# Two feed-forward stages with seven-product pairs: eight plain pairs in the first, six in the second, and another order at entry and exit

## The reference

```python
def swiglu(x, w_gate, w_up, w_down):
    return (jax.nn.silu(x @ w_gate) * (x @ w_up)) @ w_down

h = h + 0.5 * swiglu(rms_norm(h, ffn1_norm[i]), ffn1_w_gate[i], ffn1_w_up[i], ffn1_w_down[i])
# attention and retention mixer
h = h + 0.5 * swiglu(rms_norm(h, ffn2_norm[i]), ffn2_w_gate[i], ffn2_w_up[i], ffn2_w_down[i])
```

## Time and profile before

| | us |
|---|---|
| median of three runs | 1853.77 |
| the three runs | 1857.15, 1853.77, 1852.72 |
| the profiled execution | 1852.79 |
| its span | 1851.0 |

### The profile page before, as it was taken

The page is one execution under the profiler, slowest core; times in us unless marked ns, Lnnn a source line. Parts: engine busy times, 40 slices in busy tenths (PEclk is TensorE's granted clock), DMA queues, the critical chain, the costliest instruction groups (busy, mean ns, idle before and its releaser), DMA issues.

```text
span 1851.0 us, 26244 instructions
## 1 busy us (share of the span) xinstructions
PE 1815.0 (98%) x9768; PEld 1535.0 (83%) x9768; DVE 1020.3 (55%) x1619; ACT 772.6 (42%) x1226; POOL 902.6 (49%) x678
## 2 busy tenths in 40 slices
PE   9899999999999999999899999999999999999998
PEld 8699988887888667888799988888877888888887
DVE  7977776225776654245876652257655375555312
ACT  6455553232332562234455542246344444444221
POOL 5444455486766524455434454353433454444542
PEclk9999999999999999999999999999999999999999
DMA  5233333253322312322233333242212222323331
GB/s 175 80 103 103 103 111 101 68 144 113 92 80 86 103 46 80 103 92 91 79 93 114 103 103 96 79 126 80 90 59 75 90 98 92 100 92 98 94 97 51
DMA packets 55195, 175.20 MB, mean 95 GB/s; under 512 B 6400, under 2 KB 10752, under 8 KB 55088
## 3 DMA queue, kind: packets, MB, share of 16 engines
q1 hardware_dynamic: 54848, 173.37, 29.9%
q10 hardware_dynamic: 240, 0.36, 0.1%
HBM read 166.63 MB, written 2.10 MB: 91 GB/s over the span
## 4 chain that ended last, share of the span: by engine, by line
PE 90%; DVE 6%; ACT 3%; issue 1%; POOL 0%; DVEq 0%; ACTq 0%; POOLq 0%
PE acc L2033 20%; PE acc L2035 20%; PE acc L2034 20%; PE acc L2233 6%; PE acc L2234 5%; PE acc L2238 5%; PE acc L2138 1%; PE acc L2140 1%; PE acc L2139 1%; DVE comb L1375 1%; DVE aux L1386 1%; DVE comb_raw L1358 1%; PE aux L2414 1%; ACT comb_raw L870 1%; PE acc L2564 1%
## 5 line engine op out<-in xcount | busy, mean ns | idle before, releaser
L710 POOL TENSOR_TENSOR w_lo<-w_raw,w_hi 128x512 fp32r<-128x512 f32 x498 | 671.5, 1372 | 698.8 <-ACT w_hi L817 698.7
L817 ACT ACTIVATE w_hi<-w_raw 128x1024 fp32r<-128x1024 f32 (+2 forms) x249 | 254.4, 1028 | 465.1 <-PE acc L2035 397.2
L2033 PE MATMUL acc<-u_hi,w_lo 128*128 128x512 f32 x1032 | 411.6, 399 | 0.3 <-DVE gcum L1907 0.2
L2035 PE MATMUL acc<-u_hi,w_hi 128*128 128x512 f32 x1032 | 402.1, 390 | 0.0
L2034 PE MATMUL acc<-u_lo,w_hi 128*128 128x512 f32 x1032 | 401.9, 389 | 0.0
L2233 PE MATMUL acc<-comb,w_hi 128*128 128x256 f32 x896 | 228.3, 286 | 20.0 <-ACT tmp L893 11.0
L730 POOL TENSOR_TENSOR w_lo<-w_raw,w_hi 128x512 fp32r<-128x512 f32 x96 | 133.8, 1394 | 212.3 <-ACT w_hi L883 212.3
L2033 PEld LDWEIGHTS acc<-u_hi,w_lo 128*128 128x128 f32 x1032 | 193.7, 188 | 49.6 <-issue 9.1
L2034 PEld LDWEIGHTS acc<-u_lo,w_hi 128*128 128x128 f32 x1032 | 193.8, 188 | 41.3 <-issue 2.6
L2035 PEld LDWEIGHTS acc<-u_hi,w_hi 128*128 128x128 f32 x1032 | 193.7, 188 | 41.1
L2234 PE MATMUL acc<-comb,w_hi 128*128 128x256 f32 x896 | 227.2, 285 | 0.0
(11 more groups left out here) (382 smaller groups left out, 3219.2 us busy)
## 6 DMA issues: line engine op xcount, KB each, us to landing
w_raw<-in_w_up SPq DMA_DIRECT2D x132, 512.0 KB, 3.6
w_raw<-in_w_mix SPq DMA_DIRECT2D x67, 512.0 KB, 3.6
w_raw<-in_w_down SPq DMA_DIRECT2D x48, 512.0 KB, 3.5
w_raw<-in_w_gla SPq DMA_DIRECT2D x30, 512.0 KB, 3.6
w_raw<-in_w_down SPq DMA_DIRECT2D x24, 384.0 KB, 3.1
w_raw<-in_w_ple SPq DMA_DIRECT2D x10, 512.0 KB, 3.8
tmp<-tmp SPq DMA_DIRECT2D x36, 64.0 KB, 2.0
h<-in_xT SPq DMA_DIRECT2D x8, 256.0 KB, 6.2
```

The source lines that it names most:

```text
L710: ins = pool.tensor_tensor(w_lo[:, slot, part], w_raw[:, slot, part], w_hi[:, slot, part].bitcast(F32), ALU.subtract)
L817: act.activation(w_hi[:, slot, 0:width], w_raw[:, slot, 0:width], ACT.Copy).then_inc(hi_ready, 1)
L2033: pe.matmul(o, w_lo[:, slot, columns], x_hi, start=first, stop=False)
L2035: return pe.matmul(o, w_hi[:, slot, columns], x_hi, start=False, stop=last)
```

## The change

`PLAIN` becomes `(8, 6)`, one number for each stage, `EARLY` becomes 8: in FFN1 the pairs 6 and 7 are plain, in FFN2 their products go to `hid_raw` as before but are split in periods 18 and 19 (`p - LAZY`) into places of their own. 14 late blocks are left in both, and the low ones lie in another order, so that the first four wait for product s1 and the next two for s3. The last plain pair's multiplication and its two parts move from ahead of the first period into it. At the exit `right_up` comes after two late blocks.

```diff
-PLAIN = 6
-EARLY = PLAIN
+PLAIN = (8, 6)
+EARLY = 8
...
-            return late_hi[:, k - EARLY, :], late_lo[:, (k - EARLY - 4) % LATE, :]
+            i = k - EARLY
+            return late_hi[:, i, :], late_lo[:, i + 2 if i < 4 else i - 4 if i < 6 else i, :]
...
+        LAZY = KF - EARLY - 2
...
@@ ACT, ffn_up
-                    hidden_hi(p, up_t[:, p % 2, :])
+                    if p < PLAIN[f] - 1:
+                        hidden_hi(p, up_t[:, p % 2, :])
...
+                    if p == PLAIN[f]:
+                        hidden_hi(p - 1, up_t[:, (p - 1) % 2, :])
+                    if PLAIN[f] <= p - LAZY < EARLY:
+                        late_hidden(p - LAZY)
                     left_gate(p)
...
-                split_comb("g1")
-                split_comb("s1")
-                split_slabs(n0 + 11)
-                split_comb("s2")
-                split_comb("s3")
-                plain_gate(3)
-                split_slabs(n0 + 12)
+                if f == 0:
+                    split_slabs(n0 + 11)
+                    plain_gate(3)
+                    split_slabs(n0 + 12)
+                    split_comb("g1")
+                    split_comb("s1")
+                    split_slabs(n0 + 13)
+                    plain_gate(4)
+                    split_slabs(n0 + 14)
+                    split_comb("s2")
+                    split_comb("s3")
+                    split_slabs(n0 + 15)
+                    plain_gate(5)
+                    split_slabs(n0 + 16)
+                else:
...
@@ DVE, ffn_up
-                def plain_pair(p):
+                def plain_evict(p):
...
+                def plain_pair(p):
+                    plain_evict(p)
                     plain_product(p)
+                    hidden_lo(p, up_t[:, p % 2, :])
...
                 def period(p):
...
+                    else:
+                        plain_product(p - 1)
                     if more:
                         sum_low(p + 1, "s2")
+                    if p == PLAIN[f]:
+                        hidden_lo(p - 1, up_t[:, (p - 1) % 2, :])
+                    if PLAIN[f] <= p - LAZY < EARLY:
+                        hidden_lo(p - LAZY, hid_raw[:, p - LAZY - PLAIN[f], :])
                     left_gate(p)
...
-                    if EARLY + 4 <= k < EARLY + 8:
-                        dve.wait_ge(q_done, q_count(f, KF - 1, "s1"))
-                    elif k >= EARLY + 8:
-                        dve.wait_ge(tile_done, t0 + 2 * (KF - 1) + (1 if k < EARLY + 12 else 2))
-                    hidden_lo(k, hid_raw[:, k - EARLY, :])
+                    if k < EARLY + 6:
+                        dve.wait_ge(q_done, q_count(f, KF - 1, "s1" if k < EARLY + 4 else "s3"))
+                    else:
+                        dve.wait_ge(tile_done, t0 + 2 * (KF - 1) + (1 if k < EARLY + 10 else 2))
+                    hidden_lo(k, hid_raw[:, k - PLAIN[f], :])
...
-                for of in ("g2", "s4", "u2"):
-                    split_comb(of)
-                plain_pair(5)
-                for p in range(PLAIN, KF):
+                split_comb("g2")
+                plain_evict(PLAIN[f] - 1)
+                split_comb("s4")
+                split_comb("u2")
+                for p in range(PLAIN[f], KF):
                     period(p)
-                for k in range(EARLY, EARLY + 6):
-                    late_hidden(k)
+                late_hidden(EARLY)
+                late_hidden(EARLY + 1)
                 right_up(KF - 1)
-                for k in range(EARLY + 6, EARLY + 12):
+                for k in range(EARLY + 2, EARLY + 8):
                     late_hidden(k)
                 left_up(KF - 1)
                 product(KF - 1)
-                for k in range(EARLY + 12, KF):
+                for k in range(EARLY + 8, KF):
                     late_hidden(k)
```

More of the change, by code:

```diff
@@ L531, in pair_no @@
         def pair_no(f, p):
-            return f * PAIRS + p - PLAIN
+            return sum(KF - PLAIN[e] for e in range(f)) + p - PLAIN[f]
         def q_count(f, p, of):
@@ L622, in _ @@
             sp.wait_ge(lo_ready, RING)
-            for n in range(RING, 2 * PLAIN):
+            for n in range(RING, 2 * PLAIN[0]):
                 load(n, A["w_up1"][n])
@@ L663, in _ @@
                     sp.dma_start(dec[:, :], A["decay"][step[1] + 1]).then_inc(dec_loaded, 16)
-            for n in range(2 * PLAIN):
+            for n in range(2 * PLAIN[1]):
                 load(plan.first["up2"][0] + n, A["w_up2"][n])
@@ L734, in lo_pairs @@
                 n0 = plan.first[name][0]
-                for p in range(PLAIN, KF):
+                for p in range(PLAIN[f], KF):
                     pool.wait_ge(half_hi, pair_no(f, p) + 1)
                     lo_unit(name, p, "g1").then_inc(half_lo, 1)
-                    if p > PLAIN:
+                    if p > PLAIN[f]:
                         pool.wait_ge(hi_ready, n0 + 2 * p)
@@ L905, in late_hidden @@
                 def late_hidden(k):
[L906 to L907 removed]
+                    if k >= EARLY:
+                        act.wait_ge(q_done, q_count(f, KF - 1, ("g1", "s2", "g2", "s3")[(k - EARLY) // 4]))
+                    hidden_hi(k, hid_raw[:, k - PLAIN[f], :])
                 def period(p):
                     more = p + 1 < KF
[L912 removed]
+                    if p > PLAIN[f]:
                         copy_part(p - 1, 3)
@@ L955, in ffn_up @@
                 split_slabs(n0 + 10)
-                split_comb("g1")
-                split_comb("s1")
-                split_slabs(n0 + 11)
-                split_comb("s2")
-                split_comb("s3")
-                plain_gate(3)
-                split_slabs(n0 + 12)
+                if f == 0:
[13 more added lines that the diff above has]
+                else:
+                    split_comb("g1")
+                    split_comb("s1")
+                    split_slabs(n0 + 11)
+                    split_comb("s2")
+                    split_comb("s3")
+                    plain_gate(3)
+                    split_slabs(n0 + 12)
                 for of in ("g2", "s4", "u2"):
                     split_comb(of)
-                unit_hi(PLAIN, "g1", half_hi)
-                unit_hi(PLAIN, "s2", sum_hi)
-                plain_gate(4)
-                unit_hi(PLAIN, "g2", hi_ready)
-                unit_hi(PLAIN, "s3", sum_hi)
-                for p in range(PLAIN, KF):
+                unit_hi(PLAIN[f], "g1", half_hi)
+                unit_hi(PLAIN[f], "s2", sum_hi)
+                plain_gate(PLAIN[f] - 2)
+                unit_hi(PLAIN[f], "g2", hi_ready)
+                unit_hi(PLAIN[f], "s3", sum_hi)
+                for p in range(PLAIN[f], KF):
                     period(p)
@@ L980, in ffn_up @@
                 split_slabs(d0 + 3)
-                for k in range(EARLY + 12, KF - 1):
-                    late_hidden(k)
+                late_hidden(KF - 2)
                 split_slabs(d0 + 4)
@@ L1457, in ffn_up @@
                     plain_product(0)
+                    hidden_lo(0, up_t[:, 0, :])
                 else:
@@ L1463, in ffn_up @@
                 combine()
[L1464 to L1478 removed]
+                if f == 0:
+                    plain_pair(3)
+                    split_comb("g1")
+                    split_comb("s1")
+                    plain_pair(4)
+                    split_comb("s2")
+                    split_comb("s3")
+                    plain_pair(5)
+                else:
+                    split_comb("g1")
+                    plain_pair(3)
+                    split_comb("s1")
+                sums_loaded(PLAIN[f])
+                for of in ("s3", "s1", "s2", "s4"):
+                    add(PLAIN[f], of)
+                if f == 1:
+                    split_comb("s2")
+                    split_comb("s3")
+                plain_pair(PLAIN[f] - 2)
+                sum_low(PLAIN[f], "s2")
+                sum_low(PLAIN[f], "s3")
+                split_comb("g2")
+                plain_evict(PLAIN[f] - 1)
+                split_comb("s4")
+                split_comb("u2")
+                for p in range(PLAIN[f], KF):
                     period(p)
[L1480 to L1481 removed]
+                late_hidden(EARLY)
+                late_hidden(EARLY + 1)
                 right_up(KF - 1)
[L1483 removed]
+                for k in range(EARLY + 2, EARLY + 8):
                     late_hidden(k)
@@ L2200, in ffn_up @@
                     f = k // 2
-                    for j in range(RING, 2 * PLAIN):
+                    for j in range(RING, 2 * PLAIN[f]):
                         fm_tile(t0 + j, [(n0 + j, b) for b in range(KD)], u_hi, u_lo)
@@ L2270, in up_end @@
                     multiply(p, "u2", "c", False).then_inc(tile_done, 1)
-                for p in range(PLAIN, KF - 1):
+                for p in range(PLAIN[f], KF - 1):
                     bank_a(p)
-                    if p > PLAIN:
+                    if p > PLAIN[f]:
                         gate_end(p - 1)
```

53 lines of the change are left out of this document (18 added, 35 removed).

## The result

| | before | after |
|---|---|---|
| median, us | 1853.77 | 1843.93 |
| lowest to highest of five runs | 1852.72 to 1857.15 | 1842.93 to 1844.93 |
| profiled execution | 1852.79 | 1844.09 |
| its span | 1851.0 | 1842.3 |

The ratio is 0.9945, with a 95% interval of 0.993 to 0.9959. The kernel became 9.8 us faster by the medians and 8.7 by the profiled executions; 13.8 were forecast. 1843.93 lies inside the range, 3.9 us above the predicted time.

The account below looks back on a forecast made before the run. PE, busy 98% of the span, was taken as the bound. FFN1 6.3, FFN2 3.3 and exits 6.8 make 16.4 us, less one clock fall of 2.6: 13.8 gained, 1840.0 us predicted, range 1835.5 to 1846.0.

Parts of the forecast that it names:

- the case with the greatest chance: At the two FFN entries, one fall of the clock costing 2.6 us, wait before s4 3.3: 1840.0 us, chance 0.42.
- the three signs of being wrong: s4's wait at the entries 4 us or more, the down projection waits, or FFN1's plain tiles show gaps.
- What bounds the kernel: PE is busy 98% of the span; only its work and the gaps in it move the end.
- The exits: Up-bank read moved ahead of late blocks at both FFN exits: 3.4 us gained twice, 6.8.
- DVE stands waiting in FFN1: At FFN1's entry two more plain pairs leave DVE 15 us against 7 us of delay, so it waits for the last tile.
- The wait before s4 ... becomes 3.3.: PE's wait for ACT's third copy at each entry falls from 4.34 to 3.3 us; bounds 2.5 and 4.3.
- The clock: At each entry an even chance of a fall to the low level, 2.6 us for each fall; one fall counted.
- the rival that both fall: Rival: the clock falls at both FFN entries, 1842.6 us; chance 0.20.
- the entries' chain isn't shortened: Rival: at both entries the hidden block eats the 2.25 us, s4's wait stays 4.34; 1844.0 us, chance 0.06.
- POOL's pressure should be over by then: 14 late blocks at the exits and into the down projection: priced at nothing, upper bound 1.7 us twice.
- where DVE and ACT wait for PE anyway: nothing: Splitting blocks 6 and 7 in FFN2's periods 18 and 19 costs nothing.
- The sum: FFN1 6.3, FFN2 3.3, exits 6.8, together 16.4 us, less one clock fall of 2.6: 13.8 us gained.

Follow-up runs that it names:

- the fastest version: Changed kernel with the hidden block's parts a period later, splits of s4 and u2 out of the way, FFN2's down slab split held: 1830.67 us.
- the repeat: The changed kernel itself run once more, nothing changed, for its time and the clock at both entries: 1843.8 us.

## Why the prediction was right, and by how much not

The gain was forecast, and the time lies in the range. But the case with the greatest chance (one fall of the clock, a wait of 3.3) did not come, and two of the three signs of being wrong did: s4's wait is 4.02, and the down projection waits. FFN1's plain tiles show no gap.

- *What bounds the kernel: right.* What was gained and lost are gaps of PE and its clock, to within 0.2 us of the 8.7; PE's own work grew by the 1.6 us worked out. That eight plain pairs pay more than this was right too, here by 4.2 us and in the fastest version by 5.6.
- *The exits: right, by 0.3 us.* 6.5 measured for 6.8. Undoing them costs 7.7, because those waits can bring the low clock as well, which the prediction's rows did not show.
- *DVE stands waiting in FFN1: right.* 4.75 us of idle time before its last plain tile.
- *What failed: "The wait before s4 ... becomes 3.3."* It was 4.02 and 4.03. The mis-sized term is the hidden block ahead of the left gate: 1.2 us forecast (ACT 0.55, DVE 0.6), 1.7 measured by taking it away. Of these DVE waited 0.34 for ACT's high part, and its own instruction took 1.34, since POOL's subtraction of g2 had begun 0.47 us earlier; with ACT's order turned round it took 0.68. The trace of before has such an instruction at 0.69 (913.98), where POOL was still for almost all of it, and it has POOL's subtraction just where the block was to go, behind DVE's low part of s2 at 920.83:

```profile
921.39 1.26 POOL L730 TENSOR_TENSOR w_lo<-w_raw,w_hi 128x512 fp32r<-128x512 f32 x1 [3.85 <-ACT w_hi L883]
```

- *The rest of that term:* about 0.2 us of each wait lies in the additions (3.00 us, 2.91 before) and in handovers; it wasn't separated. Over both entries the wait is 1.45 us longer than forecast.
- *The clock: one fall at 2.6 forecast, two at 1.5 and 2.2 measured*, in the repeat at 1.5 and 2.4: 1.1 us more. The even chance for each entry rested on the wait being 3.3. The rival that both fall was right in this.
- *The rival that came nearest, given a chance of 0.06, was "the entries' chain isn't shortened"*, with 1844.0: the hidden block eats the 2.25 us that the earlier additions bring, and both entries fall. 1.7 of the 2.25 were eaten; the wait is 4.0 for its 4.34, FFN1 gained 4.1 for its 3.0 and FFN2 0.3 for its nothing. That its time fits to 0.1 us is luck, for it has neither the down projection's 1.9 nor the 0.5 of periods 18 and 19.
- *"POOL's pressure should be over by then": wrong in FFN2.* The late blocks cost 1.9 us there, more than the upper bound of 1.7, by the same cause as the hidden block: 8.61 us for six blocks beside POOL, 4.79 where only the first met it. The left up and the product ahead of them took 1.7 us (1076.55 to 1078.24) for the 1.1 of the bound. In FFN1 POOL stood still from 253.19 on, the six took 4.79 from 251.96, and nothing was lost.
- *"where DVE and ACT wait for PE anyway: nothing": wrong by 0.5 us.* The two blocks split in FFN2's periods stand ahead of the left gate as well, and met POOL (1.37 us).
- *The sum:* 0.3 at the exits, 1.45, 1.1, 1.9 and 0.5 make 5.25, against the 5.1 us between forecast and profiled execution.
- *A blind spot with no price:* the prediction compared the product's move only by the wait before s4. Left in its place with eight plain pairs it brings another wait, 2.2 us for the low part of s1, in both stages. It didn't hurt the forecast, for the move was made.

## What to carry to other kernels

Before you price a DVE instruction with two operands in SBUF, look for what POOL does in the same microsecond: here one such instruction on the path to the matrix engine took double, and turning round two instructions of a third engine (ACT) mended it. Where a chain of short instructions ends a wait, take out of it all that nobody waits for, even if it fits: three blocks of work that were put elsewhere (the hidden block's two parts, the splits of s4 and u2) gave 12 us, about as much as the change itself. Work that moves into periods where an engine idles isn't free either if it stands ahead of what the matrix engine waits for. And price a wait of PE with the clock that it may cost, at every place where PE waits some 3 us, not only where the low level shows in the one trace at hand.
